# The sample tile of a delta stage: two strided copies a step sooner, state loads and reads in another order, the next tile's X ahead of the residues

## The chip, the core and the metric

One core of a Trainium2 chip runs the whole program. The metric is the time of one execution in microseconds (us), the median of several runs. The engines are TensorE (PE in the rows; its weight loads PEld), VectorE (DVE), ScalarE (ACT), GpSimd (POOL) and SyncE (SP, which here issues DMAs only). They run side by side, each through its own instructions in order, and wait for one another by semaphores.

## What is computed

A two-layer decoder step for a prompt of 2048 tokens and a sample group of 8 sequences with 4 tokens each. The part that the change touches is the recurrence of the second layer, a gated delta rule in chunks:

```
def step(s, xs):
    u_n, w_n, qk_n, qd_n, kt_n, gl_n = xs
    v_new = u_n - jnp.einsum('bhcd,bhde->bhce', w_n, s)
    o = jnp.einsum('bhcd,bhde->bhce', qd_n, s) + jnp.einsum('bhij,bhje->bhie', qk_n, v_new)
    s = s * gl_n[..., None, None] + jnp.einsum('bhcd,bhce->bhde', kt_n, v_new)
    return s, o
```

`u` and `w` come out of a triangular solve in each chunk. The prompt starts from a zero state and its chunks follow one another. Each of the 8 sample sequences has a state of its own (`state_gdn`, 8 heads of 128 x 128, 512 KB), which is read, used for 4 tokens, updated and written out. Behind the recurrence come a norm, a gate, an output projection, the residual addition and the final norm.

## The kernel before

The program runs five stages one after another. The last, `layer1_delta` (line 3071), does the recurrence and all that follows it. It goes over 17 tiles of 128 rows: 16 of the prompt and one that holds the 32 sample rows. The sample tile stands at place SPOS = 8, between prompt tiles 7 and 8, so that its work can be put beside that of its neighbours.

Each engine's block is a loop `for t in range(NT + 2)` in which a step t calls functions on tiles t-2 to t+4: a tile's keys are loaded four steps ahead, normed three ahead, its triangular system is set up and solved (by GpSimd) two ahead, and its outputs are projected and added one step behind. The order of calls in the loop is written by hand, and it is the order in which an engine does them; a call that must wait holds up all calls behind it on its engine.

For a prompt tile the state of the prompt is read by line 3248 (keys) and 3258 (queries). For the sample tile, `sample_reads` (line 3392) does both for each sequence b: a matmul with the masked columns of b (`qkm[:, b]`, 64 columns: 32 for keys, 32 for queries, all zero but for the four tokens of b) as weights, and the state of b as the moving operand, all eight added up in the banks C[0] and C[1]. Five sequences are read at the start of step 8, the last three behind the first half of the projection of tile 7 (`project`, line 3387).

`qkm` is set to zero once by GpSimd; `sample_queries` (line 3761) on VectorE fills in the tokens with 16 copies of 128 x 16 at the end of step 7, behind `gated(7)` (lines 3757 and 3759).

The states of the sequences have four places, `sg[:, b % 4]`. States 0 to 3 are loaded in step 1. States 4 to 7 are loaded by SP at the start of step 8, each once the state in its place has been read (`sr_ps`). SG_ORDER updates sequences 4 to 7 first, then 0 to 3, which `sample_states` loads again as stores free their places.

Behind the reads, VectorE makes `residues` (line 3631), TensorE `solved` (3310), ScalarE copies it to `vn` (3531). TensorE then turns the X of tile 9 (`turn_x`, 3367), which VectorE's `turn_back` (3736) and `spread` (3744) make from GpSimd's solution (3878), and computes `outputs` (3331); ScalarE's `level5` (3495) and `qk_squares` (3489) come next, VectorE's `qk_sums` (3638) and `outputs` (3722). Only then does ScalarE begin the masks of `sample_masks` (3580), one for each sequence, written in turn to R and qsd. TensorE's `sample_update` (3420) multiplies keys by masked values, and VectorE (3793) adds the result to the state. The key reads of tile 9 (line 3248) wait for the last of these additions.

Some names: `turn_qk` (3342), `turn_o` (3378) and `key_products` (3348) are groups of eight on TensorE between the reads and the projection; `squares` (3483), `turned_qk` (3536) and `turned_o` (3555) stand ahead of the other work of a step on ScalarE; `add_half` (3672) adds a half of the projection to the residual; SP's `gate_rows(t+1)`, `qk_rows(t+4)` and `y1_rows(t)` load 512 KB each, the first of them once `gated(t)` is done.

## Time and profile before

| | us |
|---|---|
| median of 3 runs | 3558.45 |
| lowest, highest | 3549.77, 3564.68 |
| the profiled execution's time | 3553.13 |
| its span, first to last instruction | 3551.6 |
| TensorE busy | 3171.8 (89%) |
| VectorE busy | 1831.1 (52%) |
| ScalarE busy | 1366.9 (38%) |
| GpSimd busy | 900.5 (25%) |

The profile is one execution. A row of the order of time has a start from the span's begin, a length over all instructions merged in it, the engine, the line of the kernel, the operation, the tile written and the tile read, the shape and the count; in brackets stand the idle time of the engine ahead of it and the instruction that ended it. A float32 matmul appears as two records, so a batch of `sample_reads` has eight. The granted clock (PEclk) is a share of TensorE's full 2.4 GHz; 0.50 is 1.2 GHz. The delta stage takes the last fifth of the span; the sample tile's step lies in it between 3148 and 3247 us.

### The profile page before, as it was taken

The numbers are of one execution on the slowest core, as the hardware profiler recorded it, in microseconds if no ns is written. First come the engines' busy times: TensorE is split into PE (matmuls) and PEld (weight loads), VectorE is DVE, ScalarE is ACT, GpSimd is POOL, SyncE is SP. The second block draws the span as 40 slices with busy tenths as digits, with TensorE's granted clock in tenths as the row PEclk, the third lists the DMA queues.
The fourth block names the chain that finished last, engine by engine and source line by source line (L and its number), as shares of the span: only waits on it lengthen the run. The fifth ranks groups of instructions, "written<-read, shape, count | busy, mean of one in ns | idle before, by whom it ended". The sixth has DMA issues, their size and how long they took to land. (4 is left out here: it accounts for less than half of the span.)

```text
span 3551.6 us, 47758 instructions
## 1 busy us (share of the span) xinstructions
PE 3171.8 (89%) x15557; PEld 1740.0 (49%) x15557; DVE 1831.1 (52%) x3714; ACT 1366.9 (38%) x2789; POOL 900.5 (25%) x1776
## 2 busy tenths in 40 slices
PE   7998888999998989778669999999999968978998
PEld 4553434444444444344435444444444456646665
DVE  0000395668878888864211341531523857656663
ACT  2220114666676767676322112121121334433442
POOL 3331133322232221000000000000000467754771
PEclk9998999999999999888789999999999989987999
DMA  5556676655443333100474111021111242223211
GB/s 182 183 179 207 193 231 196 190 158 175 143 134 119 123 110 102 54 4 4 139 267 162 36 57 71 24 68 53 32 60 33 65 154 99 80 95 113 101 60 66
DMA packets 254395, 401.68 MB, mean 113 GB/s; under 512 B 47320, under 2 KB 130689, under 8 KB 251873
## 3 DMA queue, kind: packets, MB, share of 16 engines
q1 hardware_dynamic: 231652, 382.20, 33.1%
q0 software_dynamic: 4096, 8.40, 0.9%
q10 hardware_dynamic: 18432, 8.40, 0.8%
q8 instruction: 113, 1.85, 0.2%
q14 instruction: 102, 0.84, 0.1%
HBM read 318.02 MB, written 103.82 MB: 119 GB/s over the span
## 5 line engine op out<-in xcount | busy, mean ns | idle before, releaser
L2366 PE MATMUL QB<-hT,w_c 128*128 128x512 f32 x1024 | 449.3, 593 | 0.0
L724 PE MATMUL PB<-wb,hT_ahead 128*128 128x512 f32 x832 | 418.6, 629 | 26.4 <-DMA wb<-in_w_in_ab 22.2
L2366 PEld LDWEIGHTS QB<-hT,w_c 128*128 128x128 f32 x1024 | 190.1, 190 | 217.7 <-issue 217.6
L302 PE MATMUL P0A<-w_all,hT 128*128 128x512 f32 (+1 forms) x816 | 266.9, 487 | 0.0
L884 ACT COPY ptT<-PT 128x512 f32<-128x512 f32 (+3 forms) x320 | 164.3, 519 | 234.4 <-PE PT L735 233.8
L2219 PE MATMUL QA<-arena,hT 128*128 128x512 f32 (+1 forms) x768 | 250.2, 481 | 3.4 <-DVE crow L2924 2.3
L3387 PE MATMUL RPJ<-w_co,oT 128*128 128x512 f32 x544 | 248.8, 607 | 4.2 <-ACT oT L3555 3.2
L842 ACT ACTIVATE signs_out<-isc,mid 128x512 bf16<-128x512 f32 (+6 forms) x168 | 229.5, 1366 | 30.3 <-DVE mid L979 29.2
L724 PEld LDWEIGHTS PB<-wb,hT_ahead 128*128 128x128 f32 x832 | 149.6, 199 | 186.3 <-issue 158.8
L993 DVE TENSOR_SCALAR_CACHE_REDUCE band<-isc,mid 128x384 bf16<-128x384 f32 (+6 forms) x168 | 236.4, 1407 | 1.3
L735 PE MATMUL PT<-ident,sm 128*128 128x128 f32 x1088 | 187.7, 295 | 50.2 <-ACT sm L874 46.5
L2193 PE MATMUL QS<-arena 128*128 128x512 f32 x512 | 224.9, 597 | 0.7 <-ACT arena L2638 0.7
L2967 POOL TENSOR_SCALAR stat<-stat 128x1 f32<-128x1 f32 x16 | 3.1, 192 | 874.6 <-POOLq L122 874.6
L713 PE MATMUL PS<-kT,qT 64*128 64x512 f32 (+3 forms) x544 | 158.4, 599 | 65.3 <-DVE mxc L1041 64.9
L735 PEld LDWEIGHTS PT<-ident,sm 128*128 128x128 f32 x1088 | 127.0, 147 | 179.2 <-issue 82.7
L3875 POOL TENSOR_TENSOR arena<-arena 128x60 f32<-128x60 f32 (+24 forms) x465 | 167.2, 360 | 129.8 <-DVE arena L3731 95.7
L302 PEld LDWEIGHTS P0A<-w_all,hT 128*128 128x128 f32 x816 | 135.6, 191 | 130.9 <-issue 130.9
L2219 PEld LDWEIGHTS QA<-arena,hT 128*128 128x128 f32 x768 | 126.9, 191 | 125.9 <-issue 125.9
L2567 ACT COPY raw<-QB 128x512 f32<-128x512 f32 x64 | 37.5, 586 | 392.1 <-PE QB L2366 392.1
L1041 DVE CUSTOM_DVE_ANT_0 sm<-PS,mb 128x512 f32<-128x512 f32 (+3 forms) x272 | 153.9, 603 | 49.4 <-PE PS L713 48.9
L3878 POOL TENSOR_TENSOR arena<-arena 128x60 f32<-128x60 f32 (+24 forms) x465 | 169.8, 365 | 36.4
L751 PE MATMUL PO<-ptT,vst 128*64 128x128 f32 x2176 | 158.7, 286 | 20.0 <-ACT ptT L884 19.9
(520 smaller groups left out, 5261.6 us busy)
## 6 DMA issues: line engine op xcount, KB each, us to landing
wb<-in_w_in_ab SPq DMA_DIRECT2D x272, 512.0 KB, 3.8
out_c_all<-crow SPq DMA_DIRECT2D x256, 64.0 KB, 1.6
out_pr_all<-pr_out SPq DMA_DIRECT2D x17, 546.0 KB, 3.5
pra<-out_pr_all SPq DMA_DIRECT2D x16, 546.0 KB, 4.7
x_rows<-in_x_all SPq DMA_DIRECT2D x17, 512.0 KB, 5.7
out_hT_all<-hT SPq DMA_DIRECT2D x17, 512.0 KB, 2.9
arena<-out_c_all SPq DMA_DIRECT2D x17, 512.0 KB, 4.9
arena<-out_gc_rows SPq DMA_DIRECT2D x17, 512.0 KB, 3.7
```

What stands on the lines that cost most here:

```text
L302: ins = pe.matmul(PA[u % 6][:, 0:b - a], hT[:, t % 3, c, :], w_all[:, c, a:b], start=(c == 0), stop=(c == KD - 1))
L724: ins = pe.matmul(b_bank(g, n)[:, :], h_of(g)[:, 2 * q + k, :], wb[:, u % 4, k, :], start=(q == 0 and k == 0), stop=(q == 3 and k == 1))
L735: ins = pe.transpose(PT[v % 2][:, k * P:(k + 1) * P], sm[:, 2 * (r % 2) + a, c * CH + k * P:c * CH + (k + 1) * P], ident[:, :])
L842: act.activation(signs[:, 0:W], isc[:, s % 3, 0:W], ACT.Sign, bias=mid[:, s % 3:s % 3 + 1], scale=1.0, accum_out=cnt[:, s % 3:s % 3 + 1]). ...
L884: act.copy(ptT[:, v % 4, 0:w], PT[v % 2][:, 0:w]).then_inc(S["p_copied"], 1)
L993: link(dve.tensor_scalar(band[:, 0:W], isc[:, k, 0:W], m, 0.0, ALU.is_gt, ALU.add, accum_out=above_it))
L2193: ins = pe.matmul(PS[n][:, :], yT[:, c, :], w_o[:, c, n * 512:(n + 1) * 512], start=(c == 0), stop=(c == KD - 1))
L2219: ins = pe.matmul(PA[n % 2][:, 0:b - a], h, w_z[:, c, a:b], start=(c == 0), stop=(c == KD - 1))
L2366: ins = pe.matmul(PB[b % 2][:, 0:N], w_c[:, c, b * P:(b + 1) * P], hT[:, c, 0:N], start=(c == 0), stop=(c == KD - 1))
L3387: ins = pe.matmul(PJ[:, :], oT[:, c, :], w_co[:, c, n * 512:(n + 1) * 512], start=(c == 0), stop=(c == KD - 1))
L3875: link(pool.tensor_tensor(xtmp[:, 0:cl, 0:n], T[:, t % 2, j + 1:SB, j].unsqueeze(1).to_broadcast([P, cl, n]), Xs[:, t % 2, 0:cl, j:j + 1]. ...
L3878: ins = pool.tensor_tensor(Xs[:, t % 2, 0:cl, j + 1:SB], Xs[:, t % 2, 0:cl, j + 1:SB], xtmp[:, 0:cl, 0:n], ALU.subtract)
```

## The change

Seven edits, all in `layer1_delta`:

1. `qkm` gets 4 more columns for each sequence at the end of its memory (`QSTEP`), so that the tokens of all sequences lie at one stride, and `sample_queries` makes two copies, one for keys and one for queries, of 128 elements a partition each.
2. VectorE calls `sample_queries` in step 7 behind `state_update(7)` instead of behind `gated(7)`.
3. SP loads states 4 to 7 in step 7, between `qk_rows(11)` and `y1_rows(7)`, instead of at the start of step 8.
4. TensorE reads states 0 to 3 at the start of step 8 and 4 to 7 behind the half projection (before: 0 to 4 and 5 to 7).
5. VectorE makes `turn_back(9)` and `spread(9)` ahead of `residues(8)`, instead of behind `add_half(7, 0)`.
6. ScalarE writes the first mask behind `turned_x(9)`, the other seven where all eight were.
7. The memset of `qkm` covers the 4 columns more.

```diff
-        qkm = sb("qkm", [P, DB, 4, 2 * SR])
+        QSTEP = 4 * 2 * SR + DT
+        qkm_all = sb("qkm", [P, DB * QSTEP])
+        qkm = qkm_all[:, 0:DB * 4 * 2 * SR].rearrange("p (b k r) -> p b k r", b=DB, k=4)
...
             for t in range(NT + 2):
-                if t == SPOS:
-                    for b in range(SGS, DB):
-                        sp.wait_ge(S["sr_ps"], after(b - SGS + 1))
-                        state_in(b)
                 if live(t) and live(t + 1):
                     v_rows(t + 1)
...
                 if live(t + 4):
                     qk_rows(t + 4)
+                if t == SPOS - 1:
+                    for b in range(SGS, DB):
+                        sp.wait_ge(S["sr_ps"], after(b - SGS + 1))
+                        state_in(b)
                 if live(t - 1) and live(t):
                     y1_rows(t)
...
-                    sample_reads(range(0, 5))
+                    sample_reads(range(0, SGS))
...
-                    sample_reads(range(5, DB))
+                    sample_reads(range(SGS, DB))
...
-            def sample_masks():
-
-                for i, b in enumerate(SG_ORDER):
+            def sample_masks(parts):
+
+                for i in parts:
+                    b = SG_ORDER[i]
...
                 if live(t + 1):
                     turned_x(t + 1)
+                if t == SPOS:
+                    sample_masks(range(0, 1))
...
-                    sample_masks()
+                    sample_masks(range(1, DB))
...
-                for b in range(DB):
-                    for r in range(2):
-                        lo = SR * r + b * DT
-                        ins = dve.tensor_copy(qkm[:, b, :, lo:lo + DT],
-                                              qkT[SPOS % 3][:, 4 - 4 * r:8 - 4 * r, b * DT:(b + 1) * DT])
+                own_rows = qkm_all[:, :].rearrange("p (b x) -> p b x", x=QSTEP)[:, :, 0:4 * 2 * SR]
+                own_rows = own_rows.rearrange("p b (k r) -> p b k r", k=4)
+                for r in range(2):
+                    src = qkT[SPOS % 3][:, 4 - 4 * r:8 - 4 * r, 0:SR].rearrange("p k (b t) -> p b k t", t=DT)
+                    ins = dve.tensor_copy(own_rows[:, :, :, SR * r:SR * r + DT], src)
...
             for t in range(NT + 2):
+                if t == SPOS:
+                    turn_back(t + 1)
+                    spread(t + 1)
                 if live(t):
                     residues(t)
...
-                if live(t + 1):
+                if live(t + 1) and t != SPOS:
                     turn_back(t + 1)
                     spread(t + 1)
                 if prompt(t):
                     state_update(t)
+                if t == SPOS - 1:
+                    sample_queries()
...
-                if t == SPOS - 1:
-                    sample_queries()
                 if live(t - 1):
                     add_half(t - 1, 1)
...
-            pool.memset(qkm[:, :, :, :], 0.0).then_inc(S["qkm_zero"], 1)
+            pool.memset(qkm_all[:, :], 0.0).then_inc(S["qkm_zero"], 1)
```

## Rows read from the trace of the kernel before

**Rows 1.** Stretches: length, busy us (count) of PE, PEld, DVE, ACT, POOL, PEclk, DMA share, GB/s

```profile
3148.30:3247.10 98.80, 71.32 (x408) 52.42 (x409) 46.46 (x126) 25.03 (x40) 40.70 (x103) 0.74 0.37 112
3247.10:3282.90 35.80, 33.40 (x258) 23.59 (x259) 21.52 (x40) 14.95 (x34) 18.65 (x45) 0.95 0.33 118
```

**Rows 2.** TensorE in order of time, steps 7 to 10: start, length, instruction, [idle before]

```profile
3116.89 1.50 PE L3287 MATMUL RL<-arena 64*64 64x64 f32 x16 [2.26 <-DVE arena L3683]
3118.32 3.24 PE L3248 MATMUL RC<-state,arena 128*128 128x256 f32 x8
...
3159.25 11.80 PE L3401 MATMUL RC<-sg,qkm 128*64 128x256 f32 x40 [10.99 <-DVE qkm L3768]
3170.98 1.09 PE L3342 MATMUL RL<-ident_both,arena 128*128 128x128 f32 x8
...
3173.80 7.12 PE L3387 MATMUL RPJ<-w_co,oT 128*128 128x512 f32 x16
3180.84 5.39 PE L3401 MATMUL RC<-sg,qkm 128*64 128x256 f32 x24
3187.78 2.02 PE L3310 MATMUL RC<-R,arena 128*128 128x128 f32 x16 [1.54 <-DVE R L3631]
3196.88 1.97 PE L3367 MATMUL RL<-ident_both,arena 128*128 128x128 f32 x8 [7.08 <-DVE arena L3744]
3198.64 3.62 PE L3331 MATMUL RC<-vn,arena 128*128 128x128 f32 x16
...
3211.13 3.75 PE L3420 MATMUL RC<-R,kt 32*128 32x128 f32 x16 [6.51 <-ACT R L3580]
...
3218.22 6.20 PE L3387 MATMUL RPJ<-w_co,oT 128*128 128x512 f32 x8
...
3247.13 3.68 PE L3248 MATMUL RC<-state,arena 128*128 128x256 f32 x8 [1.30 <-DVE sg L3793]
...
3283.36 1.99 PE L3248 MATMUL RC<-state,arena 128*128 128x256 f32 x8
```

**Rows 3.** VectorE in order of time, steps 7 and 8

```profile
3140.37 1.22 DVE L3638 TENSOR_REDUCE arena<-arena 128x8 f32<-128x1024 f32 x1 [1.18 <-ACT arena L3489]
3141.51 1.27 DVE L3718 TENSOR_TENSOR o<-qsd,RC 128x512 f32<-128x512 f32 x2
...
3154.89 1.34 DVE L3757 TENSOR_TENSOR o<-o,arena 128x1024 f32<-128x1024 f32 x1 [1.82 <-POOL arena L3865]
...
3157.43 1.77 DVE L3768 COPY qkm<-qkT 128x16 f32<-128x16 f32 x16
...
3194.84 1.99 DVE L3744 TENSOR_TENSOR arena<-arena 128x1024 f32<-128x1024 f32 x1
...
3206.61 2.14 DVE L3722 SCALAR_TENSOR_TENSOR o<-qsd,arena,RC 32x128 f32<-32x128 f32 x8
...
3213.29 1.10 DVE L3793 SCALAR_TENSOR_TENSOR sg<-sg,eglb,RC 128x128 f32<-128x128 f32 x4
```

**Rows 4.** ScalarE in order of time, step 8

```profile
3159.82 1.06 ACT L3483 ACTIVATE sqy<-y 128x1024 bf16<-128x1024 f32 x1 [11.54 <-DVE y L3672]
...
3190.46 1.07 ACT L3531 COPY vn<-RC 128x512 f32<-128x512 f32 x2
...
3209.74 1.13 ACT L3580 ACTIVATE R<-vn,arena 32x1024 f32<-32x1024 f32 x1
```

**Rows 5.** GpSimd in order of time: the last of tile 9's solver, one of tile 10's

```profile
3164.14 0.22 POOL L3878 TENSOR_TENSOR arena<-arena 128x8 f32<-128x8 f32 x1
...
3195.05 1.83 POOL L3878 TENSOR_TENSOR arena<-arena 128x29 f32<-128x29 f32 x1
```

**Rows 6.** A stretch of one us, columns as in rows 1

```profile
3118.00:3119.00 1.00, 1.00 (x6) 0.79 (x5) 1.00 (x2) 0.52 (x1) 0.92 (x2) 0.50 0.00 0
```

**Rows 7.** SP's queue in order of time: the loads of states 4 to 7

```profile
3162.95 6.77 SPq L3183 DMA_DIRECT2D sg<-in_state_gdn  x4
```

**Rows 8.** DMA issues between 3150 and 3200: count, KB each, median us to landing

```profile
sg<-in_state_gdn SPq DMA_DIRECT2D x4, 512.0 KB, 4.5
```

## The prediction

> **What bounds the kernel now.** I read the stretches first, then TensorE's order of time through the one tile that the change touches, then the other engines beside it. The step of the sample tile, counted from the end of TensorE's work for the step before (3148.3) to the first read of the state for tile 9 (3247.1), lasts 98.8 us; the next step lasts 35.8 [rows 1]. In the long one TensorE is busy 71.3 us and its granted clock is 0.74, against 33.4 us and 0.95 in the next. So the step is a chain of waits around TensorE, and waiting also slows it. The waits are in TensorE's rows [rows 2]: 10.99 us ahead of the state reads of line 3401 until VectorE has written qkm, 1.54 us ahead of line 3310, 7.08 us ahead of the turning of X (line 3367) until VectorE's spread (line 3744), 6.51 us ahead of the state updates (line 3420) until ScalarE's first mask. Every one of them ends on a step that the change moves. TensorE's first row after the step waits for VectorE's last state update, so whatever is saved before that row moves all that follows.
>
> Durations come from the profiled execution: span 3551.6, time 3553.1 us. The median of the three runs is 3558.45, and they spread from 3549.8 to 3564.7. The sum is made against 3553.1 and carried over to the median; half a per cent, about what a measurement of this kernel can tell from no change, is 17.8 us.
>
> **Masked queries earlier, and in two copies.** Sixteen copies take 1.77 us, and stand behind the gating of tile 7, which itself waited 1.82 us for GpSimd (line 3757) and then ran to 3157.4 [rows 3]. Moved behind state_update(7) they start at about 3139.2, where VectorE next idles 1.18 us ahead of line 3638. Two copies move the same 16 x 16 elements; the trace has no copy of this shape. Their bounds are two of the old ones (2 x 0.11) and all sixteen (1.77). I take 0.5, since each carries 128 elements a partition in short runs. The idle 1.18 us hides that; at 1.77 it would push line 3638 by 0.6 us, which the 1.82 us of waiting for GpSimd absorbs. If that cover were gone the cost would be those 0.6 us. The gating doesn't get earlier, as GpSimd sets it; only what stood behind the copies does, by 1.7 us: the second half addition of tile 6, and ScalarE's squares after it, which began at 3159.82 [rows 4].
>
> A copy beside GpSimd's solver could hold GpSimd up. The row for that is line 3878 at 3195.05: 1.83 us for one small operation that began right behind VectorE's 1.99 us of line 3744 at 3194.84 [rows 3, 5], and 0.2 us for a smaller one at 3164.14. The Trainium skill says why ("SBUF — State Buffer", Who interferes with whom): VectorE's instructions with two SBUF inputs, and its fast copies, hold a port pair that GpSimd also uses, for the whole instruction. By that rule the copies, now ahead of the GpSimd chain that ends at gating, would cost that chain at most their own 0.5 us, and the sum below would be 18.2 instead of 18.7. The same rule gives back 1.6 us of the solver for tile 10, by moving the spread; the solver isn't what that step waits for.
>
> **State reads 0 to 3 start earlier.** What else they wait for (states 0 to 3, the outputs and state update of tile 7) is over by 3142.8 [rows 3]. They follow the projection that ends at 3148.26 (3159.25 less 10.99). The late reads give the cost at full clock: 24 records in 5.39 us, 0.225 each; four batches have 32 records, 7.2 us, and end at 3155.5. The 40 records of the first group took 11.80, so its low clock cost 2.8 us [rows 2].
>
> **What is late next.** turn_qk(10) takes 1.1 us, to 3156.6; then TensorE waits for the gating, and turn_o(7) runs from 3157.5 to 3158.6. ScalarE is the next hold: the half addition lets the squares begin 0.6 us behind the gating, as they now begin 0.6 us behind the copies; squares 1.25 us with their small second instruction, turned_qk(10) and turned_o(7) 1.1 us each (two copies of 128x512, as line 3531), so 3161.6 [rows 3, 4]. key_products(10) falls in between. project(7,0), 7.1 us, ends at 3168.7, and the four later batches, 7.2 us, at 3175.9. Before, the last read ended at 3186.2: 10.3 us saved at full clock. But two gaps, of 0.9 and about 1.9 us, now stand where TensorE has only transposes. The row for a gap of that size: 2.26 us idle ahead of line 3287 at 3116.89, after which the granted clock is 0.50 in 3118 to 3119 [rows 2, 6], and line 3248 takes 3.24 us instead of 1.99. A low phase thus costs between 1.25 us (that row) and 2.8 us (the first reads). I take one such phase at 1.9: **8.4 us** saved (7.5 to 10.3).
>
> **Loads of states 4 to 7.** They leave SP at 3162.95, paced by the reads over 6.77 us [rows 7]. Now they stand ahead of y1_rows(7) but still behind gate_rows(8), which waits for the gating, and qk_rows(11). So SP gets to them at about 3158.4, all four permits already there. y1_rows(7), the load moved past, leaves some 2 us later for them (0.5 us an issue); its reader stands behind residues(8) on VectorE, some 15 us later, so nothing waits. Each load landed 4.5 us after its issue [rows 8]. Bounds for the last: 3160.3 + 4.5 = 3165 and, if the four go one behind another, 3158.4 + 4 x 4.5 = 3176. State 7 is wanted at 3174.1, state 4 at 3168.7. I take no wait, as the rows overlap: four issued over 6.77 us landed in 4.5 each. The upper end costs 2 us.
>
> **Next tile's X ahead of the residues.** The solver of tile 9 ends at 3164.4 [rows 5]; turning back (under half a us) and spreading (1.99) then end at 3166.9 in VectorE time that is idle until the last reads (3175.9). residues(8), queued behind them, lose nothing. TensorE's 7.08 us ahead of line 3367 go. What is late next is outputs(8), line 3331: its input vn is copied by ScalarE until 3191.5 in the old times [rows 4], behind ScalarE's blocks. So line 3331 moves from 3198.64 to 3191.6, 7.0 us. It took 3.62 us, where line 3310 with the same 16 records took 2.02; at full clock this and the small products behind it give 2.2 us more. The idle time that went before the 3.62 is now gone, but gaps of 1.5 and 1.0 us stay, so I take half: **8.2 us** (7.0 to 9.2). The chain from there to VectorE's outputs is unchanged: ScalarE's level 5 and squares, line 3638, line 3722.
>
> **First mask ahead.** The mask of 1.13 us moves from behind out_squares(8) to behind turned_x(9). It is queued ahead of level5(9), which has line 3638 behind it; vn to 3191.5, turned_x 1.1, mask 1.13 gives 3193.7, and the product that level5 waits for comes at 3194.2 (3191.6, 2.0 for line 3331, some 0.6 for the product), so it is covered by 0.5 us (uncovered, up to 1.1 us). State update 0 then starts with o_ready instead of 2.4 us later (3208.75 to 3211.13) [rows 2 to 4]. VectorE takes the first product only after line 3709, 3646 and 3752, 4.5 us after o_ready, but TensorE and its low clock pace this part (3.75 us for 16 records), so most of it stays: **2.1 us** (0 to 5, the latter if the projection at 3218.22, 6.20 us for 8 records, gets full clock). Stores and reloads of the states follow each update in the same order, so they move along.
>
> The memset grows by 32 elements a partition at the start of the stage, beside other loads: nothing.
>
> **Sum:** 8.4 + 8.2 + 2.1 = 18.7 us. 3553.1 becomes 3534.4; on the median, 3558.45 becomes **3539.8, forecast 3540**.
>
> **Rivals.**
> (a) *TensorE's clock stays up through the gaps*: 10.3 + 9.2 + 2.1 to 5 = 21.6 to 24.5, time 3534 to 3537. For it: dense work on both sides of the gaps. Against it: the row at 3118.
> (b) *The gaps cost the clock twice*: 7.5 + 7.0 + 0 = 14.5, time 3544. The Trainium skill ("TensorE: Matmul & The Clock Gate", HAM oscillation) speaks for it: short bursts between waits start throttled again and again. The trace agrees as far as its 0.74 goes.
> (c) *The reads' second half is held by something not moved* (loads at their upper end and beyond, or ScalarE's copies), so that the reads end where they did: 8.2 + 2.1 = 10.3, time 3548.
> (d) *Slower: the clock falls at the gap at 3156 and doesn't come back before the reads end.* Price: project(7,0) doubles (+7.1), reads 4 to 7 too (+7.2), lines 3310, 3367, 3331 (+4.5), and the second projection (+3.6): 22.4, more than the 18.7 with its own 2.9 of clock losses added back (21.6), so 3559. It decides when the low phase lasts over 20 us. Against it: clock came back within the 40 records at 3159. It needs more besides to pass half a per cent.
> (e) *It doesn't do what it says*: the first reads wait for something else at 3148, or the time comes back in step 9: then what was saved is lost again, 3558. Against it: no other writer of those tiles is later than 3142.8, and step 9's loads follow the last state store as before.
>
> **How the numbers follow.** Forecast 0.50, (a) 0.18, (b) 0.14, (c) 0.08, (d) 0.05, (e) 0.05. The forecast lies only 0.9 us beyond half a per cent, so three fifths of its chance counts as faster (0.30), with (a) and a share of spread between runs: faster 0.51. (b), (c), (e) and the rest of the forecast: same 0.44. Slower 0.05, from (d). The range takes (a) with the runs' spread of some 7 us below, and (c) with 5 us above: 3527 to 3553.
>
> **What the profile after would show.** Line 3401 starts at about 3148 with no wait on qkm, 32 records in some 7.2 us; the copies lie inside VectorE's old gap before line 3638; the loads of states 4 to 7 leave at about 3158; the last read ends about 3176 to 3179; line 3367 follows line 3310 without a gap and line 3331 waits for vn; line 3420 starts with o_ready. Step 9 should begin some 19 us earlier, at about 3228. It is wrong if line 3401's second group waits for a load, if the copies delay GpSimd's line 3864, or if the granted clock in 3158 to 3176 stays at 0.5.

## The result: 0.56 per cent faster, and the profile after

The changed kernel takes 3535.76 us (median of 5 runs, 3532.1 to 3550.2), the kernel before 3561.73 us beside it (3549.8 to 3564.8). The ratio, which is taken over all the runs and not from the two medians (these alone would give 0.9927), is 0.9944, with a 95% interval of 0.9926 to 0.9962. In a second set of runs it was 0.9955 (0.9940 to 0.9970). The forecast was 3540 us and a gain of 18.7 us; the two ratios are gains of 20 and 16 us. Half a per cent lies between them, so the question on which the chances were laid is as near to even as the prediction had it.

The stretch that the prediction went by, from the end of TensorE's projection ahead of the sample reads to the first key read of tile 9, had 98.9 us before [rows 1, 2]. In the changed kernel (stretches, columns as in rows 1):

```profile
3152.90:3233.60 80.70, 68.77 (x409) 49.20 (x408) 45.82 (x110) 24.92 (x41) 40.25 (x104) 0.80 0.47 137
3233.60:3271.40 37.80, 35.55 (x264) 25.06 (x264) 22.70 (x41) 15.12 (x34) 19.39 (x47) 0.91 0.33 112
```

18.1 us are gone, against the 18.7 of the sum. TensorE in order of time (line numbers have moved by 2: 3403 is the sample reads, 3312 solved, 3369 the turning of X, 3333 outputs, 3422 the state updates, 3250 the key reads; VectorE's have moved by 5):

```profile
3152.92 7.12 PE L3403 MATMUL RC<-sg,qkm 128*64 128x256 f32 x32
...
3162.27 1.09 PE L3380 MATMUL RL<-ident_both,o 128*128 128x128 f32 x8 [1.20 <-DVE o L3764]
3165.01 2.08 PE L3350 MATMUL RL<-arena 128*128 128x128 f32 x8 [1.65 <-ACT arena L3538]
3166.88 9.17 PE L3389 MATMUL RPJ<-w_co,oT 128*128 128x512 f32 x16
3175.98 7.12 PE L3403 MATMUL RC<-sg,qkm 128*64 128x256 f32 x32
3184.64 2.02 PE L3312 MATMUL RC<-R,arena 128*128 128x128 f32 x16 [1.54 <-DVE R L3636]
3186.50 1.04 PE L3369 MATMUL RL<-ident_both,arena 128*128 128x128 f32 x8
3188.50 2.02 PE L3333 MATMUL RC<-vn,arena 128*128 128x128 f32 x16 [0.96 <-issue]
...
3196.86 3.75 PE L3422 MATMUL RC<-R,kt 32*128 32x128 f32 x16 [4.23 <-issue]
...
3203.43 2.07 PE L3422 MATMUL RC<-qsd,kt 32*128 32x128 f32 x8 [1.11 <-DVE sg L3798]
3205.42 5.33 PE L3389 MATMUL RPJ<-w_co,oT 128*128 128x512 f32 x8
...
3233.66 3.75 PE L3250 MATMUL RC<-state,arena 128*128 128x256 f32 x8 [1.30 <-DVE sg L3798]
```

The waits of 10.99 and 7.08 us [rows 2] are gone, the one of 6.51 us is 4.23, and the one of 1.54 us ahead of solved is as it was. The reads follow the projection at once, the turning of X follows solved at once. What is late next is what the prediction named: the gating (1.20 us) and ScalarE's copies (1.65 us) ahead of the projection. VectorE and SP, and the DMA issues between 3155 and 3190 (count, KB each, us to landing):

```profile
3143.84 0.39 DVE L3774 COPY qkm<-qkT 128x128 f32<-128x128 f32 x2
3145.11 1.22 DVE L3643 TENSOR_REDUCE arena<-arena 128x8 f32<-128x1024 f32 x1 [0.87 <-ACT arena L3491]
...
3194.63 2.13 DVE L3727 SCALAR_TENSOR_TENSOR o<-qsd,arena,RC 32x128 f32<-32x128 f32 x8
...
3231.26 2.25 DVE L3798 SCALAR_TENSOR_TENSOR sg<-sg,eglb,RC 128x128 f32<-128x128 f32 x8 [1.16 <-DMA sg<-in_state_gdn]
```

```profile
3163.09 7.79 SPq L3185 DMA_DIRECT2D sg<-in_state_gdn  x4
```

```profile
sg<-in_state_gdn SPq DMA_DIRECT2D x4, 512.0 KB, 8.5
```

The two copies take 0.39 us and lie in VectorE's idle time. The loads, now issued without a read between them, take 1.9 us of SP each and land after 8.5 us, not 4.5 [rows 8]; no read waits for them. New at the end of this profile is a wait of 1.16 us for the reload of a state.

One thing needs a sentence: the profiled execution took 3545.3 us, only 7.8 less than that of before, though its stretch lost 18.1. The other 10 us lie in steps that the change doesn't touch; the second profile, below, shows why.

Cut at the end of the last read and at the end of VectorE's outputs (line 3722 before), the stretch of every kernel that was run reads, in us:

| kernel | to the last read | to the outputs | to the end | stretch |
|---|---|---|---|---|
| before | 38.0 | 22.5 | 38.4 | 98.9 |
| changed | 30.2 | 13.7 | 36.9 | 80.7 |
| changed, second profile | 27.3 | 13.7 | 37.6 | 78.6 |
| reads alone | 27.3 | 21.3 | 37.8 | 86.4 |
| X ahead alone | 36.5 | 13.7 | 38.4 | 88.5 |
| first mask alone | 38.0 | 22.5 | 36.0 | 96.6 |
| sixteen copies early | 27.5 | 13.7 | 37.5 | 78.7 |
| loads back | 30.2 | 13.7 | 36.9 | 80.7 |
| squares behind | 25.4 | 13.7 | 37.4 | 76.5 |
| all reads in one group | 14.9 | 20.6 | 37.0 | 72.5 |
| solved first | 15.1 | 13.7 | 37.8 | 66.6 |
| solved first, second profile | 14.9 | 13.7 | 37.4 | 66.0 |
| projection cut | 15.2 | 13.7 | 38.2 | 67.1 |
| updates of 128 rows | 14.8 | 13.7 | 33.5 | 62.1 |

### The profile page after: what moved, and what is told of

It reads as the page before. It is cut to its first block and busy times, and to the rows that moved or that the text cites. A ratio compares the mean times of both kernels' runs of the same rounds, so it can differ in the third digit from the quotient of the medians.

```text
span 3543.7 us, 47744 instructions
## 1 busy us (share of the span) xinstructions
PE 3184.0 (90%) x15557; PEld 1749.3 (49%) x15557; DVE 1833.1 (52%) x3700; ACT 1367.0 (39%) x2789; POOL 897.8 (25%) x1776
## 5 line engine op out<-in xcount | busy, mean ns | idle before, releaser
L724 PE MATMUL PB<-wb,hT_ahead 128*128 128x512 f32 x832 | 415.2, 625 | 25.9 <-DMA wb<-in_w_in_ab 21.6
L2567 ACT COPY raw<-QB 128x512 f32<-128x512 f32 x64 | 37.5, 586 | 395.9 <-PE QB L2366 395.9
L3886 POOL TENSOR_TENSOR arena<-arena 128x60 f32<-128x60 f32 (+24 forms) x465 | 167.1, 359 | 36.4
```

What stands on the lines that cost most here:

```text
L724: ins = pe.matmul(b_bank(g, n)[:, :], h_of(g)[:, 2 * q + k, :], wb[:, u % 4, k, :], start=(q == 0 and k == 0), stop=(q == 3 and k == 1))
L3886: ins = pool.tensor_tensor(Xs[:, t % 2, 0:cl, j + 1:SB], Xs[:, t % 2, 0:cl, j + 1:SB], xtmp[:, 0:cl, 0:n], ALU.subtract)
```

## The experiments

The first eight kernels were run once each, so they are compared by the stretch in their profile and not by their time.

**The parts alone.** Three kernels hold one part each.

Reads alone (copies, reads and loads as changed, X and mask as before):

```diff
-                if t == SPOS:
-                    turn_back(t + 1)
-                    spread(t + 1)
...
-                if t == SPOS:
-                    sample_masks(range(0, 1))
```

> The changed kernel without the moved turning of X and without the first mask ahead: what is left are the two copies, the earlier reads and the loads. Measured is the stretch from the end of TensorE's projection ahead of the sample reads to the first key read of tile 9: 98.9 us before, 80.7 us in the changed kernel. Theory (the parts add up, each takes its own wait away): the reads end 7.8 us earlier than before (30.2 us after the stretch's start instead of 38.0), the rest is as before, so the stretch is 91 us. Rival (the later waits hang on something that the reads don't move, such as GpSimd or the states' loads): they grow again behind the earlier reads, and the stretch is 95 us or more.

TensorE in this kernel:

```profile
3157.39 1.16 PE L3350 MATMUL RL<-arena 128*128 128x128 f32 x8 [1.64 <-ACT arena L3538]
3158.38 7.11 PE L3389 MATMUL RPJ<-w_co,oT 128*128 128x512 f32 x16
...
3183.19 1.97 PE L3369 MATMUL RL<-ident_both,arena 128*128 128x128 f32 x8 [7.08 <-DVE arena L3747]
```

The stretch is 86.4 us, a gain of 12.5 where 7.8 was expected. The rival falls: the later wait is 7.08 us as before. Of the 4.7 us on top, 2.9 are the clock ahead of the reads' end: the same 1.6 us gap stands ahead of line 3350, but the products of line 3350 and the projection behind it take 1.16 and 7.11 us instead of the 2.08 and 9.17 of the changed kernel's first profile. Another 1.2 lie behind the reads, mostly in line 3333 (2.66 us instead of 3.62), and 0.6 in the end part.

X ahead alone (the kernel before with edit 5):

```diff
+                if t == SPOS:
+                    turn_back(t + 1)
+                    spread(t + 1)
                 if live(t):
                     residues(t)
...
-                if live(t + 1):
+                if live(t + 1) and t != SPOS:
```

> The kernel before with one part alone: VectorE's turning back and spreading of tile 9 ahead of the residues. Theory: the reads end as before, 38.0 us into the stretch, the 7 us wait ahead of the turning of X is gone, what is late next is the copy of vn on ScalarE; from the reads' end to VectorE's outputs it takes 13.7 instead of 22.5 us, and the stretch is 90 us. Rival (the wait is only handed on, as ScalarE's level 5 and VectorE's qk_sums still come late): less than 3 us from it, stretch 96 us or more.

```profile
3188.22 2.02 PE L3310 MATMUL RC<-R,arena 128*128 128x128 f32 x16 [1.54 <-DVE R L3631]
3190.08 1.04 PE L3367 MATMUL RL<-ident_both,arena 128*128 128x128 f32 x8
3192.08 2.02 PE L3331 MATMUL RC<-vn,arena 128*128 128x128 f32 x16 [0.97 <-issue]
```

From reads to outputs it takes 13.7 us instead of 22.5, as expected: the wait of 7.08 us is gone, against 0.97 us that now stand ahead of line 3331, and most of the rest is the clock that the wait had cost, since line 3367 takes 1.04 instead of 1.97 us and line 3331 2.02 instead of 3.62 [rows 2]. The other 1.5 us of this kernel's gain lie in its first reads (10.31 instead of 11.80 us), behind the same wait; they run ahead of all that waits for the moved steps, so nothing shows that the edit shortened them.

First mask alone (the kernel before with edit 6):

```diff
+                if t == SPOS:
+                    sample_masks(range(0, 1))
...
-                    sample_masks()
+                    sample_masks(range(1, DB))
```

> The kernel before with one part alone: ScalarE's first mask behind the copy of XT. Theory: the first state update of TensorE starts 0.1 us after VectorE's outputs instead of 2.4, and since TensorE at its low clock paces the updates, 1.5 to 2.1 us arrive at the end of the stretch: 97 us. Rival: VectorE, which takes the first product 4.5 us after its outputs, sets the pace, so nothing arrives: 98.9 us.

```profile
3207.35 3.75 PE L3420 MATMUL RC<-R,kt 32*128 32x128 f32 x16 [4.23 <-issue]
```

The updates start 0.1 us after the outputs, and the end part is 36.0 instead of 38.4 us: 2.3 us of the stretch, a little over the 1.5 to 2.1 that were expected.

**Which pieces of the first part matter.** Sixteen copies at the new place:

```diff
-                for r in range(2):
-                    src = qkT[SPOS % 3][:, 4 - 4 * r:8 - 4 * r, 0:SR].rearrange("p k (b t) -> p b k t", t=DT)
-                    ins = dve.tensor_copy(own_rows[:, :, :, SR * r:SR * r + DT], src)
+                for b in range(DB):
+                    for r in range(2):
+                        lo = SR * r + b * DT
+                        ins = dve.tensor_copy(qkm[:, b, :, lo:lo + DT],
+                                              qkT[SPOS % 3][:, 4 - 4 * r:8 - 4 * r, b * DT:(b + 1) * DT])
```

> The changed kernel with the masked queries as sixteen small copies, at the new place. Theory: 1.8 instead of 0.4 us fill VectorE's idle time ahead of qk_sums(10) (0.87 + 0.39 us in the changed kernel) and push it by 0.5 us, which the 1.8 us that VectorE later waits for GpSimd swallow: the stretch stays at 80.7 us, give or take 0.5. Rival: the strided form is what makes the early place free, and 0.5 us or more arrive at the gating of tile 7 and at the end.

VectorE, where the gating still waits as long for GpSimd, and then TensorE:

```profile
3144.79 1.80 DVE L3773 COPY qkm<-qkT 128x16 f32<-128x16 f32 x16
...
3160.76 1.35 DVE L3762 TENSOR_TENSOR o<-o,arena 128x1024 f32<-128x1024 f32 x1 [1.81 <-POOL arena L3873]
```

```profile
3163.43 1.09 PE L3380 MATMUL RL<-ident_both,o 128*128 128x128 f32 x8 [1.41 <-DVE o L3764]
```

The stretch is 78.7 us, that of the changed kernel's second profile. It lies 2 us under the 80.7 that was expected, because the clock stayed up behind the gap of 1.65 us, as it did in that second profile. TensorE waits 1.41 us for the gating instead of 1.20 (1.25 in the second profile): the 1.4 us of copies saved are worth 0.2 us. It is the place that counts, not the form.

Loads back at the start of SP's step 8:

```diff
-                if t == SPOS - 1:
+                if t == SPOS:
                     for b in range(SGS, DB):
                         sp.wait_ge(S["sr_ps"], after(b - SGS + 1))
                         state_in(b)
```

> The changed kernel with the loads of states 4 to 7 back at the start of SP's step 8, behind y1_rows(7). Theory: in the changed kernel SP reaches these loads only once the gating of tile 7 lets gate_rows(8) through, so the old place is at most 1 us later, and the later reads, which begin 23 us into the stretch, find their states either way: no wait ahead of the second group of reads, stretch 78.7 to 80.7 us as in the two runs that have all parts. Rival (the moved loads are what lets the reads run in two groups of four): the second group waits for a load, 2 us or more.

```profile
3161.08 0.43 SPq L3178 DMA_DIRECT2D y1t<-out_y_all  x1
3161.56 8.08 SPq L3185 DMA_DIRECT2D sg<-in_state_gdn  x4
```

The stretch is 80.7 us, and there is no wait ahead of the second reads, as expected. The loads leave 0.5 us later than they would, behind one more issue. This edit of the change is worth nothing here: gate_rows(8), ahead of both places, waits for the gating.

ScalarE's squares behind the copies of turned_o(7):

```diff
-                if live(t - 2):
+                if live(t - 2) and t != SPOS:
                     squares(t - 2)
...
                 if t == SPOS:
+                    squares(t - 2)
                     sample_query_reads()
```

> The changed kernel with ScalarE's squares of tile 6 behind the copies of turned_o(7) in step 8, instead of ahead of turned_qk(10). Theory (the gap ahead of key_products is ScalarE's, which holds turned_qk behind the squares, and these wait for VectorE's half addition): turned_qk runs while TensorE waits for the gating, the 1.65 us gap goes, the projection starts 2 to 2.5 us earlier in the stretch (11.5 instead of 13.1 to 14.0 us), and all that follows with it: reads end at 25 to 28 us, stretch 76 to 78.5 us. Rival (the gap is TensorE's own, or the next wait takes it over): no change in the start of the projection.

```profile
3158.47 1.09 PE L3380 MATMUL RL<-ident_both,o 128*128 128x128 f32 x8 [1.18 <-DVE o L3765]
3159.40 1.06 PE L3350 MATMUL RL<-arena 128*128 128x128 f32 x8
3160.35 7.13 PE L3389 MATMUL RPJ<-w_co,oT 128*128 128x512 f32 x16
```

The gap of 1.65 us ahead of line 3350 is gone, the projection starts 11.2 us into the stretch (13.1 in the second profile of the changed kernel, 14.0 in the first) and runs at full clock. The reads end at 25.4, the stretch is 76.5 us: the theory held. The squares were the next hold, at about 2 us.

**Beyond the change: what is late next, step by step.** All eight reads in one group at the start of step 8, with the loads of states 4 to 7 ahead of gate_rows(8), and X turned behind the residues again:

```diff
-                if live(t) and live(t + 1):
-                    gate_rows(t + 1)
-                if live(t + 4):
-                    qk_rows(t + 4)
                 if t == SPOS - 1:
                     for b in range(SGS, DB):
                         sp.wait_ge(S["sr_ps"], after(b - SGS + 1))
                         state_in(b)
+                if live(t) and live(t + 1):
+                    gate_rows(t + 1)
+                if live(t + 4):
+                    qk_rows(t + 4)
...
-                    sample_reads(range(0, SGS))
+                    sample_reads(range(0, DB))
...
-                if t == SPOS:
-                    sample_reads(range(SGS, DB))
...
+                if live(t):
+                    residues(t)
                 if t == SPOS:
                     turn_back(t + 1)
                     spread(t + 1)
-                if live(t):
-                    residues(t)
```

> The changed kernel with all eight reads in one group at the start of step 8, the loads of states 4 to 7 ahead of gate_rows(8) on SP, so that they leave as the reads free their places, and the residues ahead of the turning back of X. Theory: what splits the reads is only that the loads stand behind the gating; each load (4.5 us to landing) is there before its read or less than 1 us late, so the reads end 14.3 to 16 us into the stretch, the projection follows without a gap and at full clock, line 3312 starts about 25 us into the stretch instead of 29 to 31.7: stretch 73 to 76 us. Rival (loads can't keep up with the reads at 1.8 us for 512 KB): the second four reads wait 2 us each, reads end at 20 us or later, and less than 2 us is left of the gain.

```profile
3156.95 1.94 PE L3403 MATMUL RC<-sg,qkm 128*64 128x256 f32 x8 [0.53 <-DMA sg<-in_state_gdn]
```

The 64 records of the reads are through 14.9 us into the stretch, with 0.53 us of waiting for the last state, and fill the time in which TensorE had waited for the gating and for ScalarE. So the rival (reads that end at 20 us or later) falls. The stretch is 72.5 us, just under the 73 to 76 that were expected. From the last read to the outputs it now takes 20.6 us instead of 13.7: TensorE does the projection, 7.1 us, behind the reads, and the chain over solved and outputs stands behind it.

In the next kernel this chain goes first: the projection of tile 7 stands behind the query products, and on ScalarE and VectorE the tile's own steps come ahead of those of its neighbours.

```diff
-                    project(t - 1, 0, range(KD))
+                    if t != SPOS:
+                        project(t - 1, 0, range(KD))
...
                 if t == SPOS:
+                    project(t - 1, 0, range(KD))
                     sample_update(range(0, 2))
...
+                if t == SPOS:
+                    sample_query_reads()
                 if live(t + 2):
                     turned_qk(t + 2)
...
                 if t == SPOS:
-                    sample_masks(range(0, 1))
+                    blocks(t + 2)
...
                     qk_squares(t + 3)
+                if t == SPOS:
+                    sample_masks(range(0, 1))
...
                 if t == SPOS:
+                    add_half(t - 1, 0)
                     sample_update(range(0, 4))
```

> As the run with all reads in one group, and besides: the solved values, the turning of X and the outputs of the sample tile ahead of the half projection of tile 7, which then fills TensorE's wait for VectorE's outputs; on ScalarE the copies in the order of this, on VectorE the half addition of tile 7 behind out_sums. Theory: VectorE's outputs are done 29 to 32 us into the stretch instead of 41 to 44, and the rest (36 to 38 us) is as before: stretch 66 to 70 us, some 11 to 14 us less than the changed kernel. Rival (the projection only moves into the stretch of the updates, where TensorE at low clock already sets the pace): the rest grows by the 7 us of the projection, stretch 73 us or more.

VectorE's outputs, and its last state update:

```profile
3175.61 2.13 DVE L3729 SCALAR_TENSOR_TENSOR o<-qsd,arena,RC 32x128 f32<-32x128 f32 x8
...
3213.21 2.15 DVE L3800 SCALAR_TENSOR_TENSOR sg<-sg,eglb,RC 128x128 f32<-128x128 f32 x8 [1.64 <-DMA sg<-in_state_gdn]
```

The outputs are done 28.8 us into the stretch (35.5 with all reads in one group), and the projection runs while ScalarE and VectorE work on level 5, squares and outputs. The stretch is 66.6 us: the theory held. The same kernel was then timed against the kernel before:

> The kernel of the run with the solved values ahead of the half projection once more, timed. Theory: its stretch of 66.6 us against 98.9 before is worth 32 us, ratio to the kernel before 0.990 to 0.992, the same as the version with the cut projection, whose stretch was 67.1 us. Rival (part of it comes back in the steps behind, as gates and loads of tile 9 are no longer ahead): 0.993 or above.

It takes 3525.98 us (3523.8 to 3527.9), a ratio of 0.9898 (0.9883 to 0.9912), which is just under the 0.990 to 0.992 that were expected, and a stretch of 66.0.

**The end part.** Now 37.8 of 66.6 us lie behind the outputs, and VectorE's last updates wait for a reload. This kernel has SP reload states 0 to 3 ahead of the last four stores, has the first four updates in one go, and lays the second half of the projection in two pieces between the updates that follow ("projection cut" in the table):

```diff
-                for i in range(DB):
+                for i in range(SGS):
                     state_out(i)
-                    if 1 <= i <= 4:
-
-                        sp.wait_ge(S["sg_stored%d" % (i - 1)], after(16))
-                        state_in(i - 1)
+                for i in range(SGS):
+                    sp.wait_ge(S["sg_stored%d" % i], after(16))
+                    state_in(i)
+                for i in range(SGS, DB):
+                    state_out(i)
...
-                    sample_update(range(0, 2))
+                    sample_update(range(0, 4))
+                    level5_second(t + 1)
+                    project(t - 1, 1, range(0, 4))
+                    level6_first(t + 1)
+                    sample_update(range(4, 6))
+                    project(t - 1, 1, range(4, KD))
+                    sample_update(range(6, DB))
+                    continue
...
-                if live(t - 1):
-                    add_half(t - 1, 1)
                 if t == SPOS:
                     sample_update(range(4, DB))
+                if live(t - 1):
+                    add_half(t - 1, 1)
```

> As the run with the solved values ahead of the half projection, and besides: the first four state updates in one go, the second half projection of tile 7 cut so that half of it lies behind them and half between the last four, the half addition of tile 7 behind all updates, and on SP the states 0 to 3 loaded again ahead of the stores of the last four updates. Theory (the stretch from VectorE's outputs to the end, 37.8 us, is held by the projection that lies between the updates, 5.7 us of VectorE idle, and at its end by the reload of the last state, 1.6 us): 31 to 34 us of it are left, the stretch is 60 to 64 us instead of 66.6, and the time some 0.3 per cent below the 3524 us of that run. Rival (TensorE's clock, which falls in the updates' matmuls of 32 rows, sets the pace wherever the projection lies): the rest stays at 36 us or more.

```profile
3196.03 3.62 PE L3423 MATMUL RC<-qsd,kt 32*128 32x128 f32 x16
...
3201.24 6.56 PE L3390 MATMUL RPJ<-w_co,oT 128*128 128x512 f32 x8
```

No update waits for a reload any more, and yet the end part is 38.2 us and the time 3526.5 (3525.2 to 3533.5), ratio 0.9916 (0.9901 to 0.9932): the same as without the edit, so the theory of the reloads falls and the rival holds. TensorE sets the pace, at half its clock: the 16 records of an update took 1.95 us elsewhere in this part and 3.62 here, the 8 of the projection behind them 6.56, where the other 8 took 3.70.

What the slow phases have in common is that they follow runs of the state updates, whose weights and moving rows cover 32 partitions only. So the next kernel (built on the one that solves first) multiplies all 128 rows of keys and masked values; the mask is zero for the 96 rows that are not the samples':

```diff
-                            ins = pe.matmul(C[(u + 1) % 3][:, k * P:(k + 1) * P], kt[2][0:SR, h, :], vnm[i % 2][0:SR, h, :],
+                            ins = pe.matmul(C[(u + 1) % 3][:, k * P:(k + 1) * P], kt[2][:, h, :], vnm[i % 2][:, h, :],
...
-                    act.activation(flat(vnm[i % 2][0:SR]), flat(vn[0:SR]), ACT.Copy, scale=bsel[0:SR, b:b + 1])\
+                    act.activation(flat(vnm[i % 2]), flat(vn), ACT.Copy, scale=bsel[:, b:b + 1])\
```

> As the run with the solved values ahead of the half projection, but the state updates (line 3420 of the kernel before) multiply all 128 rows of the sample tile's keys and masked values instead of the 32 that count; the masks are zero in the other 96. A matmul of 32 rows took as long as one of 128 at the same clock (2.05 and 2.02 us for 16 records), and the granted clock was 0.50 through most of the updates in every run so far. Theory (the clock goes down because the work of these matmuls is small, not because of the waits between them): with 128 rows the clock stays up, the last 16 records take 2.0 instead of 3.6 us, and the part from VectorE's outputs to the end falls from 37.8 to 33 to 35.5 us; stretch 62 to 65 us. Rival (the waits between the groups bring the clock down): 16 records at the end take 3.6 us as before, and the part stays at 37 us or more.

The end part in both kernels, solved first and then with 128 rows (columns as in rows 1):

```profile
3177.70:3215.50 37.80, 34.62 (x231) 25.14 (x230) 28.84 (x84) 11.73 (x13) 23.12 (x59) 0.77 0.54 153
```

```profile
3176.50:3210.00 33.50, 27.48 (x231) 20.89 (x230) 28.66 (x83) 11.68 (x13) 22.88 (x59) 0.99 0.62 173
```

The same 231 records took 34.62 us at a granted clock of 0.77 and 27.48 at 0.99; the busy times of VectorE and ScalarE hardly differ. The rival was that the waits between the groups bring the clock down. The wait in the middle of the second update, with what follows it, solved first and then with 128 rows:

```profile
3184.86 2.07 PE L3422 MATMUL RC<-qsd,kt 32*128 32x128 f32 x8 [1.50 <-DVE sg L3800]
3186.86 5.78 PE L3389 MATMUL RPJ<-w_co,oT 128*128 128x512 f32 x8
```

```profile
3183.58 1.16 PE L3422 MATMUL RC<-qsd,kt 128*128 128x128 f32 x8 [1.68 <-DVE sg L3800]
3184.58 3.60 PE L3389 MATMUL RPJ<-w_co,oT 128*128 128x512 f32 x8
```

Behind a wait of 1.50 us the records of 32 rows ran at half clock, and the projection behind them began at it; behind a longer wait, of 1.68 us, those of 128 rows ran at full clock. The 2.07 us stand in all three profiles that solve first with 32 rows; with 128 rows there is one profile, but each of its four timed runs is faster than all five of the other kernel. So the rival falls, and the theory held. One premise in the expectation is too strong: in the kernel that solves first, five of the eight updates ran at full clock (1.95 or 2.05 us for 16 records). Over half of the saving is in the two halves of the projection among them, 3.60 and 3.70 us instead of 5.78 and 5.40.

TensorE saves 7.1 us and the end part 4.3. Most of the rest is time in which TensorE waits for VectorE's last additions: 4.05 us ahead of the key reads, where it had waited 1.69. With 128 rows, TensorE, SP and VectorE:

```profile
3210.03 3.42 PE L3250 MATMUL RC<-state,arena 128*128 128x256 f32 x8 [4.05 <-DVE sg L3800]
```

```profile
3202.11 0.58 SPq L3185 DMA_DIRECT2D sg<-in_state_gdn  x1
```

```profile
3207.73 2.15 DVE L3800 SCALAR_TENSOR_TENSOR sg<-sg,eglb,RC 128x128 f32<-128x128 f32 x8 [1.93 <-issue]
```

The additions had waited for a reload before, 1.64 us in the kernel that solves first. Here the profile names nothing that ended the 1.93 us, but the last reload was issued 5.6 us ahead of that row and the reloads landed after 5.0 us (median of four), so I read it as the reload; that was not tried by itself. The time is 3518.3 us (3515.5 to 3521.2), ratio 0.9879 (0.9862 to 0.9896), twice the gain of the change and the best that was run. Of the 10.8 us between its profiled execution and that of the kernel that solves first (timed), 3.9 lie in the stretch, 2.9 behind it and 4.0 ahead of it. All of the 4.0 lie ahead of the stage's first key read (2867.6 us after the span's start instead of 2871.8), where the two kernels do the same work; what makes them is not shown. So of the 7.7 us between the two medians, some 4 are shown to be the edit's.

**Why two profiles of the same kernel differ by 14 us.** The changed kernel again, timed once more beside the kernel before:

> The changed kernel once more, for its time beside the run above and for a second profile. Theory (its runs differ by the clock in TensorE's gap ahead of line 3289 in the plain steps, 36.1 or 37.6 us a step, which has nothing to do with the change): the sample stretch is again 78.7 to 80.8 us, the plain steps again near one of the two lengths, and the ratio to the kernel before again 0.993 to 0.996. Rival (the changed kernel lengthens the steps behind the sample tile): steps 9 to 12 at 37.6 us here too, while steps 3 to 6 ahead of it are at 36.1.

It takes 3537.6 us (3531.1 to 3550.2), with a profiled execution of 3531.1 instead of 3545.3. Its stretch is 78.6 us; TensorE at the gap that the prediction had priced:

```profile
3158.61 1.16 PE L3350 MATMUL RL<-arena 128*128 128x128 f32 x8 [1.65 <-ACT arena L3538]
3159.61 7.11 PE L3389 MATMUL RPJ<-w_co,oT 128*128 128x512 f32 x16
```

The gap is the same to a hundredth (1.65 us), and the clock doesn't fall behind it. The stretch makes 2.1 of the 14 us; 6.4 lie ahead of it, 5.6 of them in this stage's steps, and 5.6 behind it. Behind the stretch the second execution takes 304.5 us to its end, just as the kernel before does, so the saving doesn't come back there. From key read to key read, a step before SPOS takes 36.1 to 36.4 us in the kernel before (the first, 34.0, left out); in the changed kernel's first profile the four ahead of the long one take 36.9, 37.5, 37.6 and 37.5, in the second 36.1, 36.1, 36.1 and 36.3. The head of one such step, first profile and then second:

```profile
3082.53 1.96 PE L3289 MATMUL RL<-arena 64*64 64x64 f32 x16 [2.19 <-DVE arena L3688]
3084.43 3.78 PE L3250 MATMUL RC<-state,arena 128*128 128x256 f32 x8
```

```profile
3079.13 1.14 PE L3289 MATMUL RL<-arena 64*64 64x64 f32 x16 [2.24 <-DVE arena L3688]
3080.20 1.99 PE L3250 MATMUL RC<-state,arena 128*128 128x256 f32 x8
```

The same gap of 2.2 us stands ahead of line 3289 in both; behind it the key reads take 3.78 us, at half clock, or 1.99. The price is some 1.5 us a step; eight or nine such steps make the 11 us. The kernel before shows both outcomes in one execution: its row at 3116.89 has 2.26 us of idle time ahead of line 3287 and key reads of 3.24 us [rows 2], and a step earlier the same 2.26 us are followed by key reads at full clock:

```profile
3080.81 1.14 PE L3287 MATMUL RL<-arena 64*64 64x64 f32 x16 [2.26 <-DVE arena L3683]
3081.88 1.99 PE L3248 MATMUL RC<-state,arena 128*128 128x256 f32 x8
```

The edits don't decide it: with the reads alone and with 128 rows the steps ahead take 36.0 to 36.3 us, with the loads back and in the kernel of the end part most take 37.6, and the kernel that solves first has 37.5 in one profile and 36.0 in the other, from the same code. So the rival falls that the change lengthens these steps, and the spread of some 15 us over the runs of the kernel before may well have the same source, though only one of them was profiled. What decides in which of the two lengths a run's steps fall stays open.

## Why the prediction was right, point by point

- *The forecast* of 3540 lies 4 and 2 us above the two medians (3535.8 and 3537.6), and the sum of 18.7 us between what the two profiles' stretches lost, 18.1 and 20.3. The mechanism was right: the three waits that carry the sum went or shrank, and what was named as late next is what was late. That the total is within 2 us is in part luck, as the three terms below miss by up to 2.3 us and in both directions. Whether the gain passes half a per cent, the point of the chances, is still hardly to be told: the first interval ends at 0.9962, the second at 0.9970.
- *State reads earlier, 8.4 us:* 7.8 in the first profile, 10.7 in the second. The order of what is late next (gating, then ScalarE) was right. The mis-sized term is the low phase behind the gaps: taken as 1.9 us, it was 2.9 or nothing. The forecast made one price of two outcomes, which the trace of before already held (3080.81 beside 3116.89, above). For this term the second profile is rival (a), and the reads alone and the sixteen copies went its way as well, while the loads back went the other.
- *X ahead, 8.2 us:* 8.9 in both profiles (22.52 to 13.66). Line 3333 got full clock at once (2.02 us), so the upper end of the term was the right one. The trace of before had it: behind 1.54 us of gap line 3310 ran at 2.02 [rows 2]. That gap of 1.54 us is not one that the change moves, as the prediction says of all four: it follows the last read, and it is 1.54 in both profiles of the changed kernel.
- *First mask, 2.1 us:* 1.5 in the first profile and 0.7 in the second, 2.4 alone. The prediction held that VectorE's late first addition costs little, as TensorE paces this part. In the changed kernel that addition comes 5.5 us behind the outputs, not 4.5 (line 3646, ahead of it, takes 3.2 us where it took 2.2 with the mask alone), and TensorE waits for it inside the second update, 1.11 us in the first profile. In the first profile the last additions also wait 1.16 us for a reload. For the rest TensorE's clock sets the pace, as the prediction had it; that the 32 rows bring it down was shown only by the last kernel.
- *Parts and whole:* alone they give 12.5, 10.3 and 2.3, together 18.1 to 20.3. The sum of 25.1 counts some low phases twice or by chance: with the reads alone line 3333 takes 2.66 us, not 3.62, and the first reads in the run with X ahead took 1.5 us less, which nothing ties to its edit. The mask, too, is worth 0.9 to 1.7 us less beside the other parts than alone.
- *Copies:* 0.5 us forecast, 0.39 measured, in idle time as said. The gating waited 1.81 us for GpSimd even with 1.80 us of copies ahead of it, so nothing here shows the rule on the shared port that the Trainium skill states ("SBUF — State Buffer", Who interferes with whom) to cost this chain more than 0.2 us. The 1.6 us that the prediction had given back to the solver of tile 10 are there: with the spread moved, the operation that took 1.83 us [rows 5] takes 0.24 in the changed kernel (line 3886 at 3191.95).
- *Loads:* no wait, as taken, but the sizes were off. Issued back to back, four loads held SP for 7.8 us instead of 4 x 0.5, landed after 8.5 instead of 4.5, and put y1_rows(7) back by 7.8 us, not 2. What was wrong is that the length of an issue was taken from paced ones; the cover of 15 us was wide enough. The run with the loads back shows that the edit is worth nothing either way.
- *Rivals:* (b), (c), (d) and (e) were not seen: the two losses of clock that (b) needs were never both there, no read waited for a load, the clock was back at the second reads, and the second profile gives nothing back behind the stretch. As a time, (a) had 3534 to 3537, so the medians hardly part it from the forecast; its stretch, 21.6 us shorter or more, was not reached, because the mask gave less. What none of them held is the swing of some 1.5 us a step in steps that the change doesn't touch, which makes 11 us between two executions of one kernel, over half of the gain.

## What to carry to other kernels

In a stretch that is a chain of waits around one engine, list every wait with what ends it, take all of them away in one sum, and ask after each what is late next; here the sum gave 18.7 us where 18 to 20 were measured, though its terms missed in both directions, and asked three times more it gave a version at twice the gain. A moved group pays by its place, not by its form: sixteen small copies did as well as two, and putting the dependent chain first with independent work behind it did more than starting its pieces sooner. Before settling a gain of half a per cent from one profile, compare the steps that weren't touched.

## What the runs showed of the hardware

- Matmuls over 32 of 128 rows: granted clock 0.77 over the end part, against 0.99 with the same matmuls over 128 rows, and 34.6 against 27.5 us of TensorE time. Multiplying by zeros was the cheaper way. Behind a wait of 1.5 us the former ran at half clock, behind one of 1.7 us the latter at full clock.
- The same gap gives two outcomes: behind 1.65 us the clock fell or didn't (9.17 or 7.11 us for the projection), and behind 2.2 us a recurring step was 36.1 or 37.6 us long. What decides between them is not shown.
- Four loads of 512 KB issued one behind another took 1.9 us each on SP and 8.5 us to land; issued as the reads went, 4.5 us.
